# Up projection of a two-layer decoder trunk: three 256-column matmuls per weight tile in place of one of 512 and one of 256 columns

## The chip, the cores and the metric

The kernel runs on one core of a Trainium2 chip. The metric is the device time in microseconds (us). Before the change it is 2064.75 us, the median of three runs (2064.12 to 2065.49). Engine names are those of the profile: PE is the matrix engine's matmul row, PEld its weight loads, DVE is VectorE, ACT is ScalarE, POOL is GpSimd and SP the queue that issues most of the transfers.

## What is computed

A trunk of two layers on 256 tokens of width 2048, in float32. Each layer is a mixer (attention of one sort or another) with its residual add, and then this:

```python
def squared_relu_mlp(h, w_up, w_down):
    a = jnp.square(jax.nn.relu(h @ w_up))
    return a @ w_down

h = rmsnorm(x, ln_mlp_g[layer])
x = x + squared_relu_mlp(h, mlp_w_up[layer], mlp_w_down[layer])
```

`w_up` is 2048 x 8192 and `w_down` is 8192 x 2048. The change touches only `jnp.square(jax.nn.relu(h @ w_up))`.

## The kernel before

**Split operands.** The matrix engine is fed with a rounded float32 format (fp32r). To keep float32 precision each operand is split in a high part (the value rounded to that format) and a low part (what the rounding left). A product is then three matmuls: high by high, high by low and low by high. The low-by-low term is left out. In the mixer and in the down projection they are written as three matmuls of 512 columns (`piece_rows`, lines 1539 to 1541, and `product`, lines 1848 to 1850): there the activations are the stationary operand, 128 x 128, and 512 columns of weights stream.

**The up projection is the other way round** (`piece_cols`, lines 1599 to 1614): a 128 x 128 tile of the weights is stationary, and the activations stream: `h[:, k]` holds for one of the 16 slices `k` of the model dimension the high parts of 256 tokens and right behind them the low parts. The high weight tile is multiplied with all 512 columns (line 1609), so that high-by-high lands in the left half of a bank of PSUM and high-by-low in its right half. The low weight tile is multiplied with the 256 high columns only (line 1612), into the right half. The two halves of the bank are added later.

**Staging.** Each layer's MLP is cut in four blocks of 2048 hidden columns (`NB`), and the up stage of a block in four chunks `c` of 512 hidden columns. A chunk is eight pieces `j`, a piece has two slices `k`, and a slice four weight tiles `m`, taken in two groups of two (`COL_GROUPS`). So a chunk has 64 weight tiles, a block 256, and the kernel's eight blocks 2048. A chunk fills four banks, one for each `m`; two sets of four banks take turns (`up_set`).

**Behind a chunk.** ScalarE copies the four right halves to `s_buf` (`right_half`, line 966), VectorE adds the left halves to it (line 1471, which also frees the banks: `cols_read`), and takes relu and square in one operation (line 1473, `y_buf`). Then ScalarE rounds `y_buf` to the high part of `a` (line 1028) and VectorE makes the low part (line 1477), and the sums of tokens that the down projection uses follow (lines 1396 to 1401 on VectorE, line 1012 on ScalarE).

**What sets the order around it.** Every engine's program is written out by hand, and semaphores tie them. SP fetches a weight chunk of 1 MB into one of four raw slots. For each piece ScalarE makes the high half (`split_hi`, line 763) and VectorE the low half (`split_lo`, line 1068), four pieces ahead of the matmuls (`AHEAD`, as many as there are slots). PE waits for each piece on `lo_done`, and at the start of a chunk for the banks (`x_added` for chunks 0 and 1, `cols_read` of the chunk two before for chunks 2 and 3). The down stage follows with eight pieces of ordinary matmuls (chunk 0), a middle part of quads with summed weights for chunks 1 and 2, for which POOL issues the transfers (lines 678 and 687), and eight pieces more (chunk 3). Its first pieces wait for the low parts of `a` (`split_done`), four slices at a time. Everywhere the weight load of a matmul is an instruction of its own in the profile (PEld), with the matmul's line.

Of the kernel before, what the change touches and what calls it, by code (L numbers as in the profile page):

```python
# [27 lines left out]
ALU = mybir.AluOpType  # L28
ACT = mybir.ActivationFunctionType
# [3 lines left out]
T = 256  # L33
TT = T // P
D = 2048
KT = D // P
# [179 lines left out]
def up_set(c):  # L216
    return (c + 1) % 2
# [109 lines left out]
def build(nc, x, positions, ln_mix_g, ln_mlp_g, sf_w_in, sf_b_f, fox_q_g, fox_k_g, sf_w_o,  # L327
# [4 lines left out]
    with ExitStack() as ctx:  # L332
# [3 lines left out]
        def sem(name):  # L336
            return ctx.enter_context(nc.semaphore(name))
# [80 lines left out]
        s_buf = nat[:, 0].rearrange("p s (k t) -> p (s k) t", t=T)  # L418
        y_buf = nat[:, 1].rearrange("p s (k t) -> p (s k) t", t=T)
# [21 lines left out]
        psum = ctx.enter_context(nc.psum_tensor("psum", [P, 8, N], F32))  # L441
        SCORES, PROBS, OUT, TURN = psum[:, 4], psum[:, 5], psum[:, 6], psum[:, 7]
        X1, X2, X3, X4, X5, X6, X7, X8 = (psum[:, b] for b in (2, 6, 4, 7, 0, 5, 1, 3))

        def head_bank(n):

            return TURN if n % 16 >= 12 and n % 2 else OUT
# [9 lines left out]
        pieces_used = sem("pieces_used")  # L457
        r_ready = sem("r_ready")
        rows_read, cols_read = sem("rows_read"), sem("cols_read")
        right_read = sem("right_read")  # L460
        consts = sem("consts")
        const_step = sem("const_step")
        x_turned, h_hi = sem("x_turned"), sem("h_hi")
# [1 line left out]
        y_done, y_hi = sem("y_done"), sem("y_hi")  # L465
# [55 lines left out]
        def half_piece(n, which):  # L521
            kts, width = shape_of(n)
            if narrow(n):
                return narrow_piece(n)[:, :, which]
            return halves[:, n % SLOTS, which, 0:N if PIECES[n][0] == "b22" else flat(kts, width)]
# [217 lines left out]
        def _(act):  # L743
# [216 lines left out]
                        act.wait_ge(out_ready, n - 1)  # L960
                    nc.scalar.copy(o_buf[:, n % 2], head_bank(n)[:, 0:T]).then_inc(out_copied, 1)

            def right_half(set_, end):

                act.wait_ge(pieces_used, end)
                nc.scalar.copy(s_buf, psum[:, 4 * set_:4 * set_ + 4, T:2 * T]).then_inc(right_read, 1)

            def mixer(chunks, start, rows_no, norm):
                n = start
# [44 lines left out]
            def mlp_block(layer, b0):  # L1014

                base, no = block_base(layer, b0), block_no(layer, b0)
                for c in range(4):

                    for j in range(7):
                        split_hi(base + 8 * c + j + AHEAD)  # L1020
                        if c == 1 and j == 3:
                            token_sums_hi(no, 1)
                        if b0 == 0 and c == 0 and j == 2:
                            turned_x(2 * layer + 1, 3, out_bank(3))
                    right_half(up_set(c), base + 8 * c + 8)
                    split_hi(base + 8 * c + 7 + AHEAD)
                    act.wait_ge(y_done, (UP0, UP1)[layer] + 4 * b0 + c + 1)
                    nc.scalar.copy(a[:, 4 * c:4 * c + 4, 0, :], y_buf).then_inc(y_hi, 1)
                    token_sums_hi(no, c + 1 if c else 0)
                for j in range(32, BLOCK_PIECES):  # L1030
                    if base + j + AHEAD < P_END:
                        split_hi(base + j + AHEAD)
                    if j == 34:
                        token_sums_hi(no, 5)
                    for at, slot, bank in ((quad_at(7) - 1, 3, X8), (quad_at(7), 0, X1)):
                        if j == at:
                            act.wait_ge(pieces_used, base + at + 1)
                            act.wait_ge(lo_done, base + quad_at(FAST_QUADS[3]) + 2)
                            nc.scalar.copy(c_sum[:, slot], bank).then_inc(joint_copied, 1)
                    if layer == 0 and b0 == NB - 1 and j in LAST_TURNS:  # L1040
                        turned_x(2, LAST_TURNS.index(j), LAST_TURN_BANK[LAST_TURNS.index(j)])
# [12 lines left out]
        def _(dve):  # L1054
# [396 lines left out]
            def mlp_block(layer, b0):  # L1451

                base, no = block_base(layer, b0), block_no(layer, b0)
                up0 = (UP0, UP1)[layer] + 4 * b0
                for c in range(4):

                    for j in range(7):
                        split_lo(base + 8 * c + j + AHEAD)
                        if c and j == 1:
                            token_sums_lo(no, c if c > 1 else 0)  # L1460
                        if c == 1 and j == 2:
                            token_sums(no, 1)
                        if c == 1 and j == 4:
                            token_sums_lo(no, 1)
                        if b0 == 0 and c == 0 and j == 2:
                            h_split(2 * layer + 1, 3, out_bank(3))
                        if b0 == 0 and c == 1 and j == 2:
                            inverse_square(layer)
                    bank = 4 * up_set(c)
                    dve.wait_ge(right_read, up0 + c + 1)  # L1470
                    v.tensor_tensor(s_buf, psum[:, bank:bank + 4, 0:T], s_buf, ALU.add).then_inc(cols_read, 1)
                    dve.wait_ge(cols_read, up0 + c + 1)
                    v.scalar_tensor_tensor(out=y_buf, in0=s_buf, scalar=0.0, in1=s_buf, op0=ALU.max,
                                           op1=ALU.mult).then_inc(y_done, 1)
                    split_lo(base + 8 * c + 7 + AHEAD)
                    dve.wait_ge(y_hi, up0 + c + 1)
                    v.tensor_tensor(a[:, 4 * c:4 * c + 4, 1, :], y_buf, a[:, 4 * c:4 * c + 4, 0, :].bitcast(F32),
                                    ALU.subtract).then_inc(split_done, 1)
                    token_sums(no, c + 1 if c else 0)
                sums = {34: 0, 37: 1, quad_at(2) - 3: 2, quad_at(3) - 1: 3, quad_at(5) - 2: 4, quad_at(6) - 1: 5}  # L1480
                end = quad_at(8)
                joined = {end - 2: (1,), end - 1: (2, 3), end: (4, 5), end + 1: (6, 7), end + 2: (8, 9),
                          end + 3: (10, 11), end + 4: (12,)}
                ends = {39: 0, BLOCK_PIECES - 1: 3}
                for j in range(32, BLOCK_PIECES):
                    if j in ends:
                        c = ends[j]
                        final = layer == 1 and b0 == NB - 1 and c == 3
                        for tt in range(TT):
                            if final and tt == 0:  # L1490
                                dve.wait_ge(half_summed, 1)
                            else:
                                dve.wait_ge(pieces_used, base + j + 1)
                            ins = add_x(tt, c, psum[:, DOWN_BANK[c] + tt])
                            if final and tt == 0:
                                ins.then_inc(x_half, 1)
                        ins.then_inc(x_added, 1)
                    if base + j + AHEAD < P_END:
                        split_lo(base + j + AHEAD)
                    if j == 33:  # L1500
                        token_sums_lo(no, 4)
                        token_sums(no, 5)
                    if j == 35:
                        token_sums_lo(no, 5)
                    if j in sums:
                        weight_sums(layer, b0, sums[j])
                    for step in joined.get(j, ()):
                        combine(no, step, base)
                    if layer == 0 and b0 == NB - 1 and j in LAST_TURNS:
                        h_split(2, LAST_TURNS.index(j), LAST_TURN_BANK[LAST_TURNS.index(j)])  # L1510
# [14 lines left out]
        def _(pe):  # L1525
# [73 lines left out]
            def piece_cols(n, j, set_, src):  # L1599

                for i in range(2):
                    k = 2 * j + i
                    for group in COL_GROUPS:
                        for which in ((0, 1) if k == 0 else (1, 0)):
                            for m in group:
                                bank = psum[:, 4 * set_ + m]
                                cols = slice(i * N + m * P, i * N + (m + 1) * P)
                                if which == 0:
                                    last = mm(bank, half_piece(n, 0)[:, cols], src[:, k].rearrange("p s t -> p (s t)"),  # L1609
                                              start=(k == 0), stop=(k == KT - 1))  # L1610
                                else:
                                    last = mm(bank[:, T:2 * T], half_piece(n, 1)[:, cols], src[:, k, 0],  # L1612
                                              start=False, stop=False)
                return last


# [350 lines left out]
```

## Time and profile before

| | |
|---|---|
| median of three runs | 2064.75 us (2064.12 to 2065.49) |
| profiled execution, first to last instruction (span) | 2063.2 us |
| granted TensorE clock, mean | 1.000 |
| PE busy | 2056.0 us (100%), 10360 matmuls |
| PEld busy | 1745.4 us (85%) |
| DVE busy | 1455.9 us (71%) |
| ACT busy | 1099.2 us (53%) |
| HBM | 209 GB/s over the span |

For the profiled execution the profile gives no other time than its span; the span is 1.6 us under the median of the runs. Busy time of PE is taken from modelled ends: matmuls overlap in the record, so the distance from one matmul's start to the next is the figure to use for what one costs, and the "mean ns of one" of a matmul is not. Where the timeline merges several instructions of a line into one row (x2, x4), the row's time runs from the first start to the last end.

### The profile page before, as it was taken

Reading aid. Unit: us, or ns where it says so; the run is one execution under the profiler, and the core shown is the slowest. Engines: PE = TensorE matmul, PEld = TensorE weight load, DVE = VectorE, ACT = ScalarE, POOL = GpSimd, SP = SyncE. Lnnn points to the kernel's source line nnn. Section 1 sums busy time; section 2 is a strip of 40 time slices with the busy share of each in tenths; the row PEclk is TensorE's granted clock in tenths of the full one; section 3 lists DMA queues with packets and bytes.
Section 4 is the critical chain, followed back from the end, with each engine's and each line's share of the span. In section 5 each row is a group of like instructions: output and inputs, shape, how many; then the busy total and the mean of one; then the engine's idle time right before and its main releaser. Section 6 shows DMA issues by size and latency. Waiting matters only on the chain.

```text
span 2063.2 us, 26156 instructions
## 1 busy us (share of the span) xinstructions
PE 2056.0 (100%) x10360; PEld 1745.4 (85%) x10360; DVE 1455.9 (71%) x1957; ACT 1099.2 (53%) x1578; POOL 214.9 (10%) x317
## 2 busy tenths in 40 slices
PE   9999999999999999999999999999999999999999
PEld 7888888888888888888888898888888888888887
DVE  6556555566876876786697788557786696687777
ACT  5546565454544544554466676444554464454454
POOL 0000000020210120010010155001110021012010
PEclk9999999999999999999999999999999999999999
DMA  8544554685796796697575443568697588679565
GB/s 281 176 158 164 163 169 158 185 263 184 241 285 194 226 279 203 190 289 235 185 238 185 154 128 123 164 204 245 199 305 208 187 262 266 200 226 289 181 196 192
DMA packets 219986, 432.33 MB, mean 210 GB/s; under 512 B 13964, under 2 KB 20184, under 8 KB 219864
## 3 DMA queue, kind: packets, MB, share of 16 engines
q1 hardware_dynamic: 198312, 380.29, 55.5%
q0 software_dynamic: 21504, 50.34, 10.7%
q8 instruction: 83, 1.36, 0.3%
q14 instruction: 39, 0.32, 0.0%
q10 hardware_dynamic: 48, 0.02, 0.0%
HBM read 428.52 MB, written 2.10 MB: 209 GB/s over the span
## 4 chain that ended last, share of the span: by engine, by line
PE 98%; DVE 1%; ACT 0%; DMA 0%; issue 0%; SPq 0%; DVEq 0%; ACTq 0%
PE psum L1609 23%; PE psum L1539 14%; PE psum L1541 14%; PE psum L1540 14%; PE psum L1612 11%; PE psum L1850 5%; PE psum L1848 5%; PE psum L1849 5%; PE psum L1689 1%; PE psum L1776 1%; PE psum L1633 1%; PE psum L1753 0%; PE psum L1582 0%; PE psum L1777 0%; DMA raw<-in_sf_w_in 0%; PE psum L1733 0%
## 5 line engine op out<-in xcount | busy, mean ns | idle before, releaser
L1068 DVE TENSOR_TENSOR halves<-raw,halves 128x1024 fp32r<-128x1024 f32 (+1 forms) x724 | 849.9, 1181 | 447.4 <-ACT halves L763 443.3
L763 ACT CAST halves<-raw 128x1024 fp32r<-128x1024 f32 (+1 forms) x724 | 725.2, 1014 | 610.2 <-PE psum L1541 294.3
L1609 PE MATMUL psum<-h,halves 128*128 128x512 f32 x2048 | 639.0, 395 | 0.0
L1612 PEld LDWEIGHTS psum<-h,halves 128*128 128x128 f32 x2048 | 380.1, 188 | 87.6
L1612 PE MATMUL psum<-h,halves 128*128 128x256 f32 x2048 | 397.9, 278 | 0.0
L1539 PE MATMUL psum<-halves,a 128*128 128x512 f32 x828 | 325.4, 393 | 0.0
L1541 PE MATMUL psum<-halves,a 128*128 128x512 f32 x828 | 322.7, 390 | 0.0
L1540 PE MATMUL psum<-halves,a 128*128 128x512 f32 x828 | 322.3, 389 | 0.0
L1609 PEld LDWEIGHTS psum<-h,halves 128*128 128x128 f32 x2048 | 314.3, 189 | 2.8
L1539 PE MATMUL psum<-halves,h 128*128 128x512 f32 (+1 forms) x508 | 201.3, 396 | 1.0 <-DVE h L1139 1.0
L1541 PE MATMUL psum<-halves,h 128*128 128x512 f32 (+1 forms) x508 | 194.9, 384 | 0.0
L1540 PE MATMUL psum<-halves,h 128*128 128x512 f32 (+1 forms) x508 | 194.5, 383 | 0.0
L1541 PEld LDWEIGHTS psum<-halves,a 128*128 128x128 f32 x828 | 155.4, 188 | 32.8
L1539 PEld LDWEIGHTS psum<-halves,a 128*128 128x128 f32 x828 | 155.5, 188 | 31.7 <-ACT nat L830 0.4
L1540 PEld LDWEIGHTS psum<-halves,a 128*128 128x128 f32 x828 | 155.6, 188 | 31.5
L678 POOL DMA_DIRECT2D mix<-in_mlp_w_down x48 | 29.8, 637 | 1194.5 <-DVE halves L1068 1101.4
L1541 PEld LDWEIGHTS psum<-halves,h 128*128 128x128 f32 x508 | 95.3, 188 | 18.0
L1539 PEld LDWEIGHTS psum<-halves,h 128*128 128x128 f32 x508 | 95.5, 188 | 17.4 <-DVE halves L1068 1.2
L1540 PEld LDWEIGHTS psum<-halves,h 128*128 128x128 f32 x508 | 95.6, 188 | 16.2
L1849 PE MATMUL psum<-halves,a 128*128 128x512 f32 x272 | 105.8, 389 | 0.0
L1850 PE MATMUL psum<-halves,a 128*128 128x512 f32 x272 | 105.8, 389 | 0.0
L1848 PE MATMUL psum<-halves,a 128*128 128x512 f32 x272 | 105.8, 389 | 0.0
(268 smaller groups left out, 2095.9 us busy)
## 6 DMA issues: line engine op xcount, KB each, us to landing
raw<-in_mlp_w_up SPq DMA_DIRECT2D x128, 1024.0 KB, 6.3
raw<-in_mlp_w_down SPq DMA_DIRECT2D x128, 1024.0 KB, 5.3
mix<-in_mlp_w_down POOLq DMA_DIRECT2D x192, 256.0 KB, 7.0
raw<-in_sf_w_in SPq DMA_DIRECT2D x45, 1024.0 KB, 5.1
raw<-in_sf_w_o SPq DMA_DIRECT2D x16, 1024.0 KB, 5.1
raw<-in_mla_w_o SPq DMA_DIRECT2D x16, 1024.0 KB, 5.2
raw<-in_mla_w_down SPq DMA_DIRECT2D x8, 1024.0 KB, 5.3
raw<-in_mla_w_ukv SPq DMA_DIRECT2D x8, 1024.0 KB, 5.5
```

The costliest lines, as they stand in the source:

```text
L678: pool.dma_start(u[:, 0], b11).then_inc(u_loaded[m % 2], 16)
L763: nc.scalar.copy(half_piece(n, 0), raw_piece(n)).then_inc(hi_done, 1)
L1068: v.tensor_tensor(half_piece(n, 1), raw_piece(n), half_piece(n, 0).bitcast(F32), ALU.subtract)\
L1539: mm(bank, x_hi, hi[:, i], start=(k == 0), stop=False)
L1540: mm(bank, x_hi, lo[:, i], start=False, stop=False)
L1541: last = mm(bank, x_lo, hi[:, i], start=False, stop=(k == total_kts - 1))
L1609: last = mm(bank, half_piece(n, 0)[:, cols], src[:, k].rearrange("p s t -> p (s t)"), start=(k == 0), stop=(k == KT - 1))
L1612: last = mm(bank[:, T:2 * T], half_piece(n, 1)[:, cols], src[:, k, 0], start=False, stop=False)
L1633: ins = nc.tensor.transpose(psum[:, bank + i // 2, col:col + P], x_tok[:, tt, k * P:(k + 1) * P], ident[:])
L1848: mm(bank, x_hi, w_hi, start=start, stop=False)
L1849: mm(bank, x_hi, w_lo, start=False, stop=False)
L1850: return mm(bank, x_lo, w_hi, start=False, stop=stop)
```

## The change

Each weight tile is now multiplied by three matmuls of 256 columns, all into the same 256 columns of PSUM: high weights by high activations, high weights by low activations, low weights by high activations. The two tiles of a group share one bank (two times 256 columns), so a chunk takes two banks instead of four. Only the first matmul into a bank carries the start flag. ScalarE reads the result through a relu (and so frees the banks), VectorE squares what ScalarE wrote, and the operation that added the halves is gone.

```diff
+        def up_bank(set_):
+
+            return psum[:, 4 * set_:4 * set_ + 2].rearrange("p b (m t) -> p (b m) t", t=T)
...
-            def right_half(set_, end):
+            def rectify(set_, end):
 
                 act.wait_ge(pieces_used, end)
-                nc.scalar.copy(s_buf, psum[:, 4 * set_:4 * set_ + 4, T:2 * T]).then_inc(right_read, 1)
+                nc.scalar.activation(s_buf, up_bank(set_), ACT.Relu).then_inc(cols_read, 1)
...
-                    right_half(up_set(c), base + 8 * c + 8)
+                    rectify(up_set(c), base + 8 * c + 8)
...
-                    bank = 4 * up_set(c)
-                    dve.wait_ge(right_read, up0 + c + 1)
-                    v.tensor_tensor(s_buf, psum[:, bank:bank + 4, 0:T], s_buf, ALU.add).then_inc(cols_read, 1)
                     dve.wait_ge(cols_read, up0 + c + 1)
-                    v.scalar_tensor_tensor(out=y_buf, in0=s_buf, scalar=0.0, in1=s_buf, op0=ALU.max,
-                                           op1=ALU.mult).then_inc(y_done, 1)
+                    v.tensor_tensor(y_buf, s_buf, s_buf, ALU.mult).then_inc(y_done, 1)
...
                     for group in COL_GROUPS:
-                        for which in ((0, 1) if k == 0 else (1, 0)):
+                        for w, x in ((0, 0), (0, 1), (1, 0)):
                             for m in group:
-                                bank = psum[:, 4 * set_ + m]
+
+                                out = up_bank(set_)[:, m]
                                 cols = slice(i * N + m * P, i * N + (m + 1) * P)
-                                if which == 0:
-                                    last = mm(bank, half_piece(n, 0)[:, cols], src[:, k].rearrange("p s t -> p (s t)"),
-                                              start=(k == 0), stop=(k == KT - 1))
-                                else:
-                                    last = mm(bank[:, T:2 * T], half_piece(n, 1)[:, cols], src[:, k, 0],
-                                              start=False, stop=False)
+                                last = mm(out, half_piece(n, w)[:, cols], src[:, k, x],
+                                          start=(k == 0 and m == group[0] and (w, x) == (0, 0)),
+                                          stop=(k == KT - 1 and m == group[-1] and (w, x) == (1, 0)))
```

## Rows read from the trace of the kernel before

**Rows 1.** The page: span, busy time, the chain that ended last by engine.

```profile
span 2063.2 us, 26156 instructions
PE 2056.0 (100%) x10360; PEld 1745.4 (85%) x10360; DVE 1455.9 (71%) x1957; ACT 1099.2 (53%) x1578; POOL 214.9 (10%) x317
PE 98%; DVE 1%; ACT 0%; DMA 0%; issue 0%; SPq 0%; DVEq 0%; ACTq 0%
```

**Rows 2.** Windows: one up stage, then one down stage (engines' busy time, clock, DMA).

```profile
581.65:670.86 89.21, 89.21 (x513) 77.88 (x512) 57.59 (x65) 40.97 (x42) 5.06 (x7) 1.00 0.71 220
670.86:753.86 83.00, 83.00 (x367) 68.72 (x366) 70.58 (x82) 46.42 (x50) 12.12 (x17) 1.00 0.78 244
```

**Rows 3.** Waits of PE (waiter, releaser: us in total, times, longest).

```profile
PE psum L1620 <- POOL ident L631: 1.6, 1, 1.6
PE psum L1539 <- DVE h L1139: 1.0, 1, 1.0
PE psum L1689 <- DVE mix L1239: 0.6, 1, 0.6
PE psum L1689 <- DVE mix L1262: 0.4, 1, 0.4
```

**Rows 4.** Timeline, PE in an up stage (start us, us, engine, line).

```profile
584.66 0.62 PE L1609 MATMUL psum<-h,halves 128*128 128x512 f32 x2
...
601.85 0.40 PE L1612 MATMUL psum<-h,halves 128*128 128x256 f32 x2
602.08 0.63 PE L1609 MATMUL psum<-h,halves 128*128 128x512 f32 x2
602.55 0.39 PE L1612 MATMUL psum<-h,halves 128*128 128x256 f32 x2
602.78 0.62 PE L1609 MATMUL psum<-h,halves 128*128 128x512 f32 x2
```

**Rows 5.** Timeline, PE: a run of 384-column matmuls in the second mixer.

```profile
1159.50 0.33 PE L1539 MATMUL psum<-halves,h 128*128 128x384 f32 x1
...
1161.41 0.33 PE L1541 MATMUL psum<-halves,h 128*128 128x384 f32 x1
```

**Rows 6.** Timeline, PE: four 256-column matmuls in a row, in two chunks.

```profile
409.75 0.63 PE L1612 MATMUL psum<-h,halves 128*128 128x256 f32 x4
410.21 0.62 PE L1609 MATMUL psum<-h,halves 128*128 128x512 f32 x2
...
432.92 0.64 PE L1612 MATMUL psum<-h,halves 128*128 128x256 f32 x4
433.40 0.62 PE L1609 MATMUL psum<-h,halves 128*128 128x512 f32 x2
```

**Rows 7.** Timeline, weight loads: sixteen before matmuls of only 8 columns.

```profile
161.76 1.86 PEld L1593 LDWEIGHTS psum<-ident,nat 16*128 16x128 f32 x16
```

**Rows 8.** Timeline, PE: 512-column matmuls after short ones in the first mixer.

```profile
89.36 0.40 PE L1540 MATMUL psum<-halves,h 128*128 128x512 f32 x1
...
90.98 0.39 PE L1541 MATMUL psum<-halves,h 128*128 128x512 f32 x1
```

**Rows 9.** Timeline, ACT behind a chunk of the up stage.

```profile
431.96 1.01 ACT L966 COPY nat<-psum 128x1024 f32<-128x1024 f32 x1 [1.68 <-PE psum L1609]
435.53 1.05 ACT L1028 CAST a<-nat 128x1024 fp32r<-128x1024 f32 x1 [1.60 <-DVE nat L1473]
```

**Rows 10.** Timeline, DVE behind the same chunk.

```profile
433.01 1.22 DVE L1471 TENSOR_TENSOR nat<-psum,nat 128x1024 f32<-128x1024 f32 x1 [1.47 <-ACT nat L966]
434.27 1.23 DVE L1473 SCALAR_TENSOR_TENSOR nat<-nat 128x1024 f32<-128x1024 f32 x1
435.41 1.22 DVE L1068 TENSOR_TENSOR halves<-raw,halves 128x1024 fp32r<-128x1024 f32 x1
436.61 1.23 DVE L1477 TENSOR_TENSOR a<-nat,a 128x1024 fp32r<-128x1024 f32 x1
```

**Rows 11.** Groups by line on ACT: the table loads.

```profile
L775 ACT ACT_TABLE_LOAD x1 | 1.3, 1283 | 1.3 <-PEq L1957 1.3
L998 ACT ACT_TABLE_LOAD x1 | 1.3, 1283 | 0.0
```

More of the change, by code:

```diff
@@ L459, in build @@
         rows_read, cols_read = sem("rows_read"), sem("cols_read")
-        right_read = sem("right_read")
         consts = sem("consts")
```

## Prediction

> **What bounds the kernel now.** I read the page first: PE is busy for the whole span and makes 98% of the chain of work that ended last, while DVE stands at 71% and ACT at 53% [rows 1]. Busy time of PE alone proves little, so I read the waits next. PE waits for 3.6 us in all, in the start and in the mixers, and not once in an up stage [rows 3]. The granted clock is 1.00 in the up and in the down stage, the higher of the two levels, 2.4 GHz [rows 2]. So in the up stage nothing but the matrix engine's own stream counts. What an edit takes off DVE or ACT is worth nothing there, and what it adds to a matmul is paid in full.
>
> The price of a matmul is the distance between starts, not its duration in the record. Before the change one up stage lasts 89.21 us [rows 2]; it has 256 weight tiles, so one tile, a 512-column and a 256-column matmul, costs **348.5 ns**. The timeline says the same: from the pair of 512s at 584.66 to that at 602.78 are 26 repeats of two 512s and two 256s, 18.12 / 26 = 697 ns for two tiles [rows 4]. There are eight such stages: 8 x 256 = 2048 tiles, 713.7 us, a third of the kernel.
>
> **The change, part by part.**
>
> *The matmuls.* The streamed columns stay the same, 768 per tile. At 2.4 GHz they take 320 ns, so 28.5 ns of a tile is something else: 14 ns for each of its two matmuls. The change makes three matmuls and three weight loads of it. Everything hangs on what a 256-column matmul costs in an unbroken stream of its kind, which this trace does not have. Four readings bound it.
>
> (a) A down stage, only 512-column matmuls, has 366 in 83.00 us, 226.8 ns each [rows 2]. A run of 384-column ones has 11 steps in 1.91 us, 173.6 ns each [rows 5]. The difference is 53.2 ns for 128 columns, near the 53.3 of the clock, so on top of the columns there is a fixed part of about 13 ns a matmul. Carried to 256 columns: 173.6 - 53.2 = 120.4 ns.
>
> (b) At the first slice of each chunk four 256-column matmuls stand in a row: 0.46 us in one chunk and 0.48 us in the next, for four [rows 6]. That is 115 and 120 ns each, 117.5 on average. A row of four leans on its neighbours at both ends, so it is not a steady rate.
>
> (c) The remainder of the mix: 697 less two 512s at 226.8 leaves 243.4 for two 256s, 121.7 ns each. This is the upper end of what I take as likely.
>
> (d) In the mix itself a pair of 256s goes from 602.55 to 602.78, and one from 601.85 to 602.08: 115 ns each [rows 4]. It is the lower end. The 512s beside them (602.08 to 602.55 for two) then take 235 ns, more than in (a), so part of the 256s' cost seems to stand in their gaps.
>
> I take **119 ns**, the middle between (a) and (b), which are nearest to the new stream: the one is a steady stream of another width, the other the right width without being steady. Three of them make 357.0 ns a tile, 8.5 ns more than now; times 2048 this is **+17.4 us**. With (b) alone it is 352.5, +4.0 ns, +8 us; with (c) 365.1, +16.6 ns, +34 us.
>
> The Trainium skill, "TensorE: Matmul & The Clock Gate", section "Back-to-back issue gap", gives for a stream of warm matmuls the columns over 2.4 plus 2.5 ns. By that a 512 costs 215.8 and a 256 109.2 ns, a third matmul adds 2.5 ns a tile, and the change would cost only 5.1 us, an estimate of 2069.9 us. This case's trace does not agree: its 512s stand 226.8 ns apart [rows 2], so the measured fixed part goes into the sum.
>
> *The weight loads.* 2048 more of them. Sixteen loads before matmuls too short to matter take 1.86 us from the first start to the last end; less one load's own 0.19 us (as the others on the timeline show) that is 15 steps of 111 ns [rows 7]. A 256-column matmul that takes 117 to 121 ns covers this, by 6 to 10 ns only. Before the change every second load had a 512 over it. I cost it at nothing; if the cover failed, the load's distance would be the floor.
>
> *Accumulation in one place.* The same 256 columns of PSUM are now added to at every second matmul. In the down stage consecutive matmuls add to the same bank at 226.8 ns with no sign of a stall [rows 2]; cost nothing. The two banks that come free are not used by anybody.
>
> *ScalarE.* The copy of 1.01 us [rows 9] becomes a relu of as many elements; I take 1.01 to 1.1 us. It now frees the banks itself, 1.3 us earlier than the add does. PE waits for them only one chunk (22 us) later and does not wait today, so nothing is gained.
>
> *VectorE.* The add, 1.22 us, goes; the square takes 1.22 like the operation it replaces [rows 10]. 32 chunks x 1.22 = 39 us less DVE busy time. The chain behind a chunk (copy, add, square, round, low half) gets about 1.25 us shorter. Who needs its end? The down stage, whose seventh piece is the first to read the last chunk's slices, 6 pieces of 12 matmuls at 226.8 ns = 16.3 us after the chunk's end; the chain today is through 5.9 us after the copy starts (431.96 to 436.61 + 1.23). Nothing waits for it, so both savings are worth nothing; if a run should show PE waiting there, that cover was misjudged. VectorE's wait is now on ScalarE's relu in place of ScalarE's copy, at the same point of its program; the low half of a weight piece is queued behind it, as it was, and PE has pieces in hand.
>
> *Sum.* The profiled execution has 2063.2 us of span; 2063.2 + 17.4 = 2080.6. The median of the runs lies 1.6 us above that span, so I predict **2082.2 us**.
>
> **The rivals.**
>
> *The 256s cost what they show in the mix (same).* If the 115 to 116 ns of (d) are a true rate, three of them are 345 to 348 ns against 348.5, and the kernel stays at 2064.75 less 0 to 7 us; at 116 it is 2063.7. For it: all the pairs of the up stage show it. Against: then the 512s beside them would cost 8 ns more than in a down stage, without a reason. Chance 0.12.
>
> *The load distance rules (faster).* In a stream of equal 256s there is no 512 to disturb the rhythm, and the matmul could follow the next load at 111 ns [rows 7]. A tile then takes 334 ns, 14.6 less, and the kernel 29.9 us less: 2034.9. It decides from 116.2 ns a matmul downwards, today's tile over three. For it: the four in a row come down to 115 in one sighting. Against: it would need the fixed 13 ns of (a) to shrink to less than 5. Chance 0.08. The skill's same page, section "LDWEIGHTS (loading the stationary operand)", puts a load at its 128 columns over 1.2, 107 ns, whatever the matmul; the trace's 111 ns distance is near that.
>
> *A broken rhythm (much slower).* After short matmuls the 512s run for a while at 231 ns (seven steps in 1.62 us) before they settle at 227 [rows 8]. If loads that are only just covered keep the stream in that state, a 256 costs 120.4 + 4.6 = 125 ns, a tile 375, and the kernel +54 us: 2119. The price is paid at every matmul. For it: the load's cover is thin. Against: the four in a row. Chance 0.07.
>
> *Relu is not in the loaded table set.* Then the change does not simply swap a copy for a relu: a table load costs 1283 ns [rows 11], and where log and exp tables alternate with it there would be some. Even two a chunk, 82 us in all, would go on an ACT that is busy 41 of 89 us in an up stage [rows 2], and PE would not feel it. It changes ACT's row, not the time. Chance that it shows in the time 0.02.
>
> **How the numbers follow.** The forecast's own case, a fixed part per matmul with 117 to 122 ns for a 256, has 0.71 and runs from 2072 to 2100 us. The range takes in this and the first rival, 2063 to 2101; left out are the load distance and the broken rhythm, 0.15 together. A measurement of this kernel can tell 0.2%, 4.1 us, from no change. Slower by more: 0.71 and 0.07, 0.78. Faster by more: 0.08 from the load distance and 0.01 from the lower edge of the first rival, 0.09. The same: 0.11 from the rest of that rival and 0.02 from the tables, 0.13.
>
> **What would show it.** In the changed profile an up stage (89.21 us before) should last 256 x 0.357 = 91.4 us, the three new groups of the up line together 6144 matmuls about 119 ns apart, and the down stage its 83.0 us as before. PE should still wait for nothing in the up stages. DVE's busy time should fall by 39 us, ACT's stay within 5 us, and the chain behind a chunk be one operation shorter. The count of table loads should stay at three. I am wrong if the up stage is at or under 89.2 us (the cost is not per matmul), if the matmuls stand 111 to 113 ns apart, or if the added time lies anywhere else than in the up stages.

## Result and profile after

The changed kernel takes **2091.09 us** (median of four runs, 2089.8 to 2094.23), the kernel before, run beside it, 2065.12. The ratio is 1.0129, with a 95% interval of 1.0117 to 1.0141: 26.0 us slower. That is in the predicted range and of the predicted sign, but 8.6 us over the predicted sum of 17.4.

The page of the changed kernel: span, busy time, and the chain that ended last by engine.

```profile
span 2088.9 us, 30220 instructions
PE 2080.7 (100%) x12408; PEld 1860.1 (89%) x12408; DVE 1420.8 (68%) x1925; ACT 1102.9 (53%) x1578; POOL 214.9 (10%) x317
PE 97%; DMA 1%; DVE 1%; ACT 1%; issue 0%; POOL 0%; ACTq 0%; POOLq 0%; DVEq 0%
```

There are 2048 more matmuls and loads than in [rows 1], and DVE has lost 35 us. The matrix engine is still the chain, with one new thing in it: 1% DMA.

Windows of the same up stage and the down stage behind it, in the changed kernel:

```profile
586.11:678.26 92.15, 92.15 (x769) 92.15 (x768) 54.41 (x62) 41.20 (x42) 5.26 (x8) 1.00 0.70 215
678.26:761.25 82.99, 82.99 (x369) 68.70 (x367) 69.75 (x82) 46.69 (x50) 12.32 (x18) 1.00 0.78 244
```

The up stage has 92.15 us against 89.21 [rows 2], the down stage is the same. 92.15 us over 256 tiles is 360.0 ns a tile, over 768 matmuls **120.0 ns** each. Weight loads are now in flight for all of the stage. One chunk's timeline shows the stream without a break:

```profile
454.73 10.48 PE L1608 MATMUL psum<-h,halves 128*128 128x256 f32 x86
```

Over eight stages, 2.94 us more each, that is 23.5 us. The spans of the two profiles differ by 25.7 us (2063.2 and 2088.9), so 2.2 us are left. They lie in the first and the third down stage, 2.2 and 0.6 us longer than before, with small differences elsewhere. There the matrix engine has waits of a kind that it had nowhere before [rows 3]:

```profile
PE psum L1538 <- DVE halves L1071: 2.1, 2, 1.9
PE psum L1617 <- POOL ident L634: 1.6, 1, 1.6
PE psum L1686 <- DVE mix L1242: 0.6, 1, 0.6
PE psum L1686 <- DVE mix L1265: 0.4, 1, 0.4
```

The first line is new; on the other side the wait of 1.0 us for `h` [rows 3] is not in this profile. The timeline of PE at the end of the first block's down stage shows the longer of its two waits:

```profile
572.59 0.39 PE L1539 MATMUL psum<-halves,a 128*128 128x512 f32 x1
572.81 0.39 PE L1540 MATMUL psum<-halves,a 128*128 128x512 f32 x1
575.05 0.50 PE L1538 MATMUL psum<-halves,a 128*128 128x512 f32 x1 [1.85 <-DVE halves L1071]
```

From 572.81 to 575.05 are 2.24 us in place of 0.23; at the other place, two blocks later, 0.61 us stand in place of 0.23, so the two cost 2.4 us. VectorE is named, but it waited for ScalarE, and ScalarE for a transfer. ACT at that place in the changed kernel:

```profile
572.70 1.99 ACT L766 CAST halves<-raw 128x1024 fp32r<-128x1024 f32 x2 [8.96 <-DMA raw<-in_mlp_w_down]
```

And in the kernel before:

```profile
568.03 2.00 ACT L763 CAST halves<-raw 128x1024 fp32r<-128x1024 f32 x2 [6.56 <-DMA raw<-in_mlp_w_down]
```

There too ScalarE waited for that load. VectorE's low half of the piece, and the first matmul that needed it, in the kernel before:

```profile
569.12 1.23 DVE L1068 TENSOR_TENSOR halves<-raw,halves 128x1024 fp32r<-128x1024 f32 x1 [4.40 <-ACT halves L763]
```

```profile
570.77 0.39 PE L1539 MATMUL psum<-halves,a 128*128 128x512 f32 x1
```

The piece was ready at 570.35 (569.12 + 1.23) and the matrix engine came to it at 570.77: in time by 0.4 us. In the changed kernel the engine would have come to it at 573.04 (572.81 + 0.23), 2.3 us later, but the load landed 4.7 us later (572.70 against 568.03). Why it lost 2.4 us more than the stages moved isn't shown. In both kernels POOL's transfers for the next block run beside it; here in the changed kernel:

```profile
558.22 0.54 POOL L681 DMA_DIRECT2D mix<-in_mlp_w_down  x1 [5.24 <-DVE halves L1071]
...
559.27 1.85 POOL L690 DMA_DIRECT2D mix<-in_mlp_w_down  x2
563.63 1.76 POOL L690 DMA_DIRECT2D mix<-in_mlp_w_down  x2 [2.51 <-DMA mix<-in_mlp_w_down]
```

Behind a chunk, DVE in the changed kernel:

```profile
433.07 1.22 DVE L1473 TENSOR_TENSOR nat<-nat 128x1024 f32<-128x1024 f32 x1 [1.58 <-ACT nat L969]
434.21 1.22 DVE L1071 TENSOR_TENSOR halves<-raw,halves 128x1024 fp32r<-128x1024 f32 x1
435.41 1.23 DVE L1476 TENSOR_TENSOR a<-nat,a 128x1024 fp32r<-128x1024 f32 x1
```

The add of [rows 10] is gone and the low half of `a` starts 2.34 us after the square instead of 3.60 us after the add: the chain is shorter by one operation, as planned. What that is worth is measured below ("The evacuation alone"). ScalarE's groups show the relu at 1025 ns where the copy took 1013 to 1016, and there are still three table loads in all (two of them here):

```profile
L969 ACT ACTIVATE nat<-psum 128x1024 f32<-128x1024 f32 x32 | 32.8, 1025 | 56.9 <-PE psum L1608 56.9
L778 ACT ACT_TABLE_LOAD x1 | 1.3, 1283 | 1.3 <-PEq L1954 1.3
L1001 ACT ACT_TABLE_LOAD x1 | 1.3, 1283 | 0.0
```

### The profile page after: what moved, and what is told of

It reads as the page before. It is cut to its first block, busy times and chain, and to the rows that moved or that the text cites. A ratio compares the mean times of both kernels' runs of the same rounds, so it can differ in the third digit from the quotient of the medians.

```text
span 2088.9 us, 30220 instructions
## 1 busy us (share of the span) xinstructions
PE 2080.7 (100%) x12408; PEld 1860.1 (89%) x12408; DVE 1420.8 (68%) x1925; ACT 1102.9 (53%) x1578; POOL 214.9 (10%) x317
## 4 chain that ended last, share of the span: by engine, by line
PE 97%; DMA 1%; DVE 1%; ACT 1%; issue 0%; POOL 0%; ACTq 0%; POOLq 0%; DVEq 0%
PE psum L1608 35%; PE psum L1538 14%; PE psum L1540 14%; PE psum L1539 14%; PE psum L1846 5%; PE psum L1845 5%; PE psum L1847 5%; DMA raw<-in_mlp_w_down 1%; PE psum L1686 1%; PE psum L1773 1%; PE psum L1630 1%; DVE halves L1071 0%; PE psum L1750 0%; PE psum L1581 0%; PE psum L1774 0%; PE psum L1730 0%
## 5 line engine op out<-in xcount | busy, mean ns | idle before, releaser
L766 ACT CAST halves<-raw 128x1024 fp32r<-128x1024 f32 (+1 forms) x724 | 728.4, 1013 | 678.1 <-PE psum L1540 297.3
L1608 PE MATMUL psum<-h,halves 128*128 128x256 f32 x6144 | 739.0, 283 | 0.0
L1608 PEld LDWEIGHTS psum<-h,halves 128*128 128x128 f32 x6144 | 738.4, 192 | 0.6
L681 POOL DMA_DIRECT2D mix<-in_mlp_w_down x48 | 29.8, 638 | 1218.3 <-DVE halves L1071 1123.7
L690 POOL DMA_DIRECT2D mix<-in_mlp_w_down x96 | 86.5, 1079 | 119.3 <-DMA mix<-in_mlp_w_down 118.8
L766 ACT CAST halves<-heads 128x1024 fp32r<-128x1024 f32 x48 | 50.5, 1053 | 45.9 <-PE psum L1847 19.2
```

Of the source, the lines that this page charges most:

```text
L681: pool.dma_start(u[:, 0], b11).then_inc(u_loaded[m % 2], 16)
L690: pool.dma_start(u[:, i], b12, accum_op=ALU.add).then_inc(u_summed[m % 2], 16)
L766: nc.scalar.copy(half_piece(n, 0), raw_piece(n)).then_inc(hi_done, 1)
L1608: last = mm(out, half_piece(n, w)[:, cols], src[:, k, x], start=(k == 0 and m == group[0] and (w, x) == (0, 0)), stop=(k == KT - 1 and m = ...
```

## Experiments

Two theories stood against each other at the start. Mine: every matmul carries a fixed part of 13 ns and the third one is all that costs. The other: the time comes with what else is new, the accumulation in one place and one bank, or the work of ScalarE and VectorE.

### The split alone

The banks, the add and everything else stay as before; only the 512 columns go in two matmuls.

```diff
                                 if which == 0:
-                                    last = mm(bank, half_piece(n, 0)[:, cols], src[:, k].rearrange("p s t -> p (s t)"),
-                                              start=(k == 0), stop=(k == KT - 1))
+                                    for x in range(2):
+                                        last = mm(bank[:, x * T:(x + 1) * T], half_piece(n, 0)[:, cols], src[:, k, x],
+                                                  start=(k == 0 and x == 0), stop=(k == KT - 1 and x == 1))
```

> The kernel before with its 512-column matmul of each weight tile split into two of 256 columns, into the same left and right halves of the same four banks; ScalarE's copy, VectorE's add and the rest stay. If the added time is a fixed part of each matmul (my theory), the up line stands 120 ns apart as in the changed kernel, the up stages take 737 us in all against 714, and the time is 2086 to 2092 us. If the time comes from adding up in one place of PSUM, or from two tiles in one bank, it is gone here: 2065 us, with 116 ns steps. If it comes from the new ScalarE and VectorE operations, it is gone too: 2065 us.

Measured: 2090.09 us, ratio 1.0123 (1.011 to 1.0137). One up stage of it (window), then its waits and the timeline of PE around the late load:

```profile
588.23:680.38 92.15, 92.15 (x770) 92.15 (x768) 56.58 (x63) 41.04 (x42) 3.65 (x5) 1.00 0.69 210
```

```profile
PE psum L1539 <- DVE halves L1068: 2.1, 1, 2.1
```

```profile
575.58 0.50 PE L1539 MATMUL psum<-halves,a 128*128 128x512 f32 x1 [2.15 <-DVE halves L1068]
575.91 0.58 PE L1540 MATMUL psum<-halves,a 128*128 128x512 f32 x1
...
577.15 0.63 PE L1540 MATMUL psum<-halves,a 128*128 128x512 f32 x1
577.58 0.63 PE L1541 MATMUL psum<-halves,a 128*128 128x512 f32 x1
```

The same 92.15 us, and the same wait at the same place. So the loss comes with the split, 25.4 us here against 26.0 in the change; one place in PSUM, relu and square have no measurable part in it. In this profile the granted clock fell behind the wait: the 512s stand 0.43 us apart instead of 0.23, and the clock of that stretch is 0.50, the 1.2 GHz level, where it was 1.00 before the wait:

```profile
576.00:579.00 3.00, 3.00 (x9) 2.32 (x8) 2.96 (x5) 2.00 (x2) 0.00 (x0) 0.50 1.02 379
```

Seven matmuls start in these 3 us, where thirteen would at 226.8 ns. The changed kernel's own profile has the wait without the fall. And the fall doesn't need the wait: the profile of the next run, "The evacuation alone", has one at 163.94 us, in the first mixer, where the engine waited for nothing but had run, from 160.99 us on, sixteen matmuls of 8 columns:

```profile
160.99 1.95 PE L1588 MATMUL psum<-ident,nat 16*128 16x8 f32 x16
```

```profile
164.00:167.30 3.30, 3.30 (x10) 2.56 (x9) 1.67 (x6) 0.65 (x3) 0.00 (x0) 0.50 0.12 44
```

The kernel before has the same sixteen matmuls [rows 7] and no fall in its profile. Such falls are a likely part of the spread between single runs, of the kernel before too (2064.12 to 2066.07 us); that the slowest run of the change (2094.23 us, mean clock 0.999) had one is not shown.

### The evacuation alone

```diff
-                nc.scalar.copy(s_buf, psum[:, 4 * set_:4 * set_ + 4, T:2 * T]).then_inc(right_read, 1)
+                nc.scalar.activation(s_buf, psum[:, 4 * set_:4 * set_ + 4, T:2 * T], ACT.Relu).then_inc(cols_read, 1)
...
-                    dve.wait_ge(right_read, up0 + c + 1)
-                    v.tensor_tensor(s_buf, psum[:, bank:bank + 4, 0:T], s_buf, ALU.add).then_inc(cols_read, 1)
...
-                    v.scalar_tensor_tensor(out=y_buf, in0=s_buf, scalar=0.0, in1=s_buf, op0=ALU.max,
-                                           op1=ALU.mult).then_inc(y_done, 1)
+                    v.tensor_tensor(y_buf, s_buf, s_buf, ALU.mult).then_inc(y_done, 1)
```

> The kernel before with the matmuls untouched, but ScalarE reads the right halves through a relu and frees the banks, VectorE's add is left out and it squares with a product. The left halves are not added, so high-by-high is missing from the result. My theory: all of this is hidden behind the matrix engine; 2065 us within 2, with 39 us less DVE busy time and the up stages unchanged at 714 us. Rival: the shorter chain behind a chunk or the earlier free banks help, 2060 us or less; or the relu costs table loads and time, over 2069 us.

Measured: 2064.63 us, ratio 0.9999 (0.999 to 1.0008). The result lacks high by high, so only its time counts. Its window of the up stage, and its page:

```profile
582.52:671.73 89.21, 89.21 (x514) 77.91 (x512) 54.27 (x62) 41.37 (x42) 5.14 (x7) 1.00 0.72 221
```

```profile
PE 2057.7 (100%) x10360; PEld 1747.4 (85%) x10360; DVE 1420.3 (69%) x1925; ACT 1104.1 (53%) x1578; POOL 215.0 (10%) x317
```

89.21 us to the hundredth, with 36 us less on VectorE. That half of the change is worth nothing here, neither way.

### Half of the slices

```diff
-                                if which == 0:
-                                    last = mm(bank, half_piece(n, 0)[:, cols], src[:, k].rearrange("p s t -> p (s t)"),
-                                              start=(k == 0), stop=(k == KT - 1))
+                                if which == 0 and k % 2:
+                                    for x in range(2):
+                                        last = mm(bank[:, x * T:(x + 1) * T], half_piece(n, 0)[:, cols], src[:, k, x],
+                                                  start=False, stop=(k == KT - 1 and x == 1))
+                                elif which == 0:
+                                    last = mm(bank, half_piece(n, 0)[:, cols], src[:, k].rearrange("p s t -> p (s t)"),
+                                              start=(k == 0), stop=False)
```

> The kernel before with the 512-column matmul split into two of 256 in every second slice only: half the added matmuls of the split alone. A fixed part per matmul is paid by the piece: the up stages gain 11.8 us (three of 120 ns against 348.5 in half the tiles), 726 us in all, and the time is 2076 to 2079 us. If the added time came from a lost rhythm that needs an unbroken stream of 256s, it would be under 5 us; if mixing widths costs more by itself, over 15 us.

Measured: 2076.92 us, ratio 1.0062 (1.0046 to 1.0077), 12.1 us over the kernel before at its side. Its window of an up stage:

```profile
582.84:673.49 90.65, 90.65 (x642) 84.97 (x640) 57.85 (x65) 41.12 (x42) 5.31 (x8) 1.00 0.70 219
```

1.44 us more than before, 2.94 for all slices: half the added matmuls, half the time. The price is per added matmul, and an unbroken stream of 256s is not needed for it.

### How near is the weight load?

```diff
-                                    last = mm(bank[:, T:2 * T], half_piece(n, 1)[:, cols], src[:, k, 0],
-                                              start=False, stop=False)
+                                    for t in range(2):
+                                        last = mm(bank[:, T + t * P:T + (t + 1) * P], half_piece(n, 1)[:, cols],
+                                                  src[:, k, 0, t * P:(t + 1) * P], start=False, stop=False)
```

> The kernel before with the 256-column matmul of the low weights split into two of 128 columns: the same number of matmuls as in the changed kernel. If only the fixed part of 13 ns counts, a tile is 226.8 + 2 x 66.6 = 360 ns and the time 2089 us. If weight loads can't follow each other faster than 111 to 112 ns, a tile is 226.8 + 2 x 112 = 451 ns, 102 more than now, and the time about 2275 us; then the 256-column matmuls of the change are 8 ns clear of that floor. If part of a load hides under the 512 beside it, between the two.

Measured: 2286.59 us, ratio 1.1077 (1.1062 to 1.1092). Two rows of its timeline are one pattern, four 128-column matmuls and two of 512. Behind them stand the weight loads of the first pattern's 128s and of the next two 512s:

```profile
499.60 0.68 PE L1609 MATMUL psum<-h,halves 128*128 128x512 f32 x2
500.12 0.56 PE L1613 MATMUL psum<-h,halves 128*128 128x128 f32 x4
500.52 0.68 PE L1609 MATMUL psum<-h,halves 128*128 128x512 f32 x2
...
501.43 0.68 PE L1609 MATMUL psum<-h,halves 128*128 128x512 f32 x2
```

```profile
499.89 0.65 PEld L1613 LDWEIGHTS psum<-h,halves 128*128 128x128 f32 x4
500.45 0.30 PEld L1609 LDWEIGHTS psum<-h,halves 128*128 128x128 f32 x2
```

From 499.60 to 501.43 are two patterns, 1.83 / 4 = 457 ns a tile. Less 226.8 for the 512 it leaves 115 ns for each 128-column matmul, where the fixed part alone would give 66.6. The two loads of the last row take 0.30 us; less one load's own 0.19 that is 0.11 us from start to start. Taken singly, the loads of this run's up projection stand 108 to 112 ns apart wherever nothing holds them longer, and none is closer. So a second limit stands beside the fixed part, the distance of the loads. The 256s of the change lie above it, 120.0 against 112, but a 128-column split falls on it: as many matmuls as the change, and 222 us lost, not 24.

### One place, back to back

```diff
-                        for w, x in ((0, 0), (0, 1), (1, 0)):
-                            for m in group:
+                        for m in group:
+                            for w, x in ((0, 0), (0, 1), (1, 0)):
```

> The changed kernel with its three matmuls of a tile one behind the other: each adds to the same 256 columns as the one before, and the high weight tile is loaded twice in a row. If accumulation into one place costs nothing even back to back and a repeated load is neither saved nor dearer, all steps stay at 120 ns and the time at 2091 us within 2. If a matmul must wait for the one before it at the same address, steps grow by tens of ns, over 2110 us. If the repeated load were left out, a step of every three would be shorter than 120 ns, under 2085 us.

Measured: 2091.18 us, ratio 1.0129 (1.0116 to 1.0143). Its window of an up stage and its weight loads as a group:

```profile
584.01:676.17 92.16, 92.16 (x770) 92.15 (x768) 54.06 (x62) 41.22 (x42) 4.94 (x7) 1.00 0.70 215
```

```profile
L1608 PEld LDWEIGHTS psum<-h,halves 128*128 128x128 f32 x6144 | 738.4, 192 | 0.6
```

Adding to the place the matmul before wrote costs nothing, and the same weights are loaded a second time: 6144 loads, none left out. The late load of the change is in this profile too, at two other block ends (2.6 us in all, the longer 2.38 us from start to start), and no fall of the clock.

### The late weight load

The transfers that POOL issues early for the next block now wait until the block before is through. The same edit was made in the changed kernel and in the kernel before.

```diff
-                    pool.wait_ge(lo_done, base - BLOCK_PIECES + quad_at(FAST_QUADS[m + 4]) + 2)
+                    pool.wait_ge(lo_done, base)
```

> The changed kernel, but the first summed-weight transfers that POOL issues for a block wait until the last piece of the block before has been split, so they no longer run beside the last down-projection chunk's own loads. The changed kernel's profile has 23.5 us more in its up stages and 2.4 us of waits of the matrix engine for a late weight load at two block ends. If those waits come from the two streams of transfers sharing the DMA engines, they are gone here: 2088.5 us, 1.5 to 3 us less than the change, and the distances of the up line stay at 120 ns. If they come from elsewhere (a slot freed late, the longer up stage itself), the time stays at 2090 to 2092 us.

> The same edit in the kernel before, which shows no such wait in its profile. 2064.7 us within 1.5, unless its other runs hold waits that the profiled one hasn't: then up to 1 us less. If the later transfers come too late for VectorE's weight sums instead, more than 2067 us.

Measured: 2087.79 us for the change with the edit (2087.62 to 2088.28, ratio to before 1.0113, 1.0099 to 1.0127), and 2064.39 for the kernel before with it (0.9999, 0.999 to 1.0008). The timeline of ACT in the edited change, where the wait was:

```profile
568.19 1.05 ACT L766 CAST halves<-raw 128x1024 fp32r<-128x1024 f32 x1 [1.61 <-PE psum L1540]
570.97 1.05 ACT L766 CAST halves<-raw 128x1024 fp32r<-128x1024 f32 x1 [1.72 <-PE psum L1540]
```

The transfers between 555 and 575 us, first in the changed kernel and then in the edited one (queue: packets, MB, share of the 16 DMA engines; and a load of 1 MB, median us from issue to landing). q0 is missing where POOL issues nothing, so it has POOL's transfers:

```profile
q0 software_dynamic: 793, 1.73, 41.8%
q1 hardware_dynamic: 1339, 2.68, 36.7%
raw<-in_mlp_w_down SPq DMA_DIRECT2D x2, 1024.0 KB, 14.1
```

```profile
q1 hardware_dynamic: 2469, 4.93, 69.6%
raw<-in_mlp_w_down SPq DMA_DIRECT2D x2, 1024.0 KB, 6.2
```

And the window of the up stage in the edited change:

```profile
584.31:676.47 92.16, 92.16 (x770) 92.15 (x769) 53.01 (x60) 41.20 (x42) 8.62 (x12) 1.00 0.74 222
```

ScalarE waits for the matrix engine again and not for a transfer, and the matrix engine has no such wait left. The change now costs 22.9 us against the kernel before at its side, and 23.4 against the kernel before with the same edit: the 23.5 us of its matmuls and no more. The interval of this ratio overlaps with that of the change, so the time alone is weak evidence; but all four runs lie under the fastest of the change (2089.8 us), and the profile has no late load. So the rest, some 3 us of 26, came from POOL's transfers beside the due loads: with them on the DMA engines a load of 1 MB took 14.1 us to land, without them 6.2. The kernel before doesn't gain; in its profile that load was just in time.

### Two attempts to beat both

Steady streams of 226.8 and 120.0 ns would make 346.8 ns a tile, where the kernel before takes 348.5. Two orders of the same matmuls were tried for it. Runs of eight:

```diff
-COL_GROUPS = ((0, 1), (2, 3))
+COL_GROUPS = ((0, 1, 2, 3),)
...
-                        for which in ((0, 1) if k == 0 else (1, 0)):
+                        for which in ((0, 1) if k % 2 == 0 else (1, 0)):
```

> The kernel before with all four tiles of a slice in one group and the order high/low turned round from slice to slice, so that eight matmuls of one width stand in a row where two did; the matmuls are the same. In the kernel before, two 512s and two 256s take 697 ns where steady streams (226.8 and the 120.0 of the changed kernel) would take 693.6. If each change of width costs 1.7 ns, three fewer a slice over 512 slices take off 2.6 us: 2062.5 us, up stages 711 us. If a 256 beside 512s simply costs 121.7 however they are ordered, nothing changes: 2065 us, 714 us.

Measured: 2065.86 us, ratio 1.0006 (0.9997 to 1.0015). One by one:

```diff
-                        for which in ((0, 1) if k == 0 else (1, 0)):
-                            for m in group:
+                        for m in group:
+                            for which in ((0, 1) if k == 0 else (1, 0)):
```

> The kernel before with the two matmuls of a tile one behind the other, so that 512 and 256 columns take turns singly (low weights first, then high), where they took turns in pairs; the matmuls are the same. Runs of eight did not lower the up stages (715 us against 714), because the 512s after a change of width run 5 to 10 ns over their steady 226.7 for several matmuls. If that surcharge needs a few equal matmuls to build up, single turns come nearer to the steady sum of 346.7 ns a tile: up stages about 711 us, the time 2062 to 2063 us, and this would beat both kernels. If every change of width costs the same, twice the changes cost 3.5 us more: 2068 us. If the mix costs 697 ns for two tiles whatever its order, 2065 us.

Measured: 2073.07 us, ratio 1.0044 (1.003 to 1.0058). The windows of an up stage, runs of eight and then one by one:

```profile
581.20:670.58 89.38, 89.38 (x513) 78.66 (x512) 57.71 (x65) 41.01 (x42) 5.18 (x7) 1.00 0.71 221
```

```profile
581.55:671.98 90.43, 90.43 (x514) 78.45 (x512) 57.45 (x64) 41.09 (x42) 4.89 (x7) 1.00 0.70 217
```

The timeline of the runs of eight:

```profile
599.82 2.00 PE L1609 MATMUL psum<-h,halves 128*128 128x512 f32 x8
601.66 1.12 PE L1612 MATMUL psum<-h,halves 128*128 128x256 f32 x8
602.61 2.00 PE L1609 MATMUL psum<-h,halves 128*128 128x512 f32 x8
```

Eight 256s take 0.95 us, 119 ns each, but the eight 512s 1.84, 230 ns each, 3 over their steady rate. Both expectations of a gain fell, and 2073 us lies above all three cases that the last one named. Mixing has a price over 346.8 ns: 1.7 ns a tile in pairs, 2.3 in eights (89.38 / 256 = 349.1), and 6.4 one by one (353.2). It is no fixed price for each change of width: eights have a quarter of the changes of pairs and cost no less. The pairs of the kernel before are the best of the three, and none of the versions tried is faster than it. What in the engine makes the 512s slower after a change of width stays open.

## Why the prediction was right, and where it fell short

**The bound** was right for the up stage: there nothing counts but the matrix engine's stream, and the third matmul is paid in full. The evacuation alone at 0.9999 shows it for the other half of the change.

**The price of a 256** was taken as 119 ns, the middle between reading (a), two steady streams of other widths, 120.4, and reading (b), four in a row, 117.5. It is 120.0. Reading (a) was right and needed no averaging. A row of 256s beside 512s is no steady rate: in the runs of eight the 256s stand 119 ns apart while the 512s take 3 ns more. The step "I take 119" is the mis-sized term: 11.5 ns a tile instead of 8.5, 23.5 us instead of 17.4. Reading (a) alone would have given 12.7 ns a tile and 26.0 us, the measured total to the tenth, but by luck: 2.5 us of it would have stood for the late loads. A slip beside it: 117 to 122 ns give 2070 to 2101 us by the prediction's own sum, where it has 2072 to 2100; the result is inside both.

**Reading (c)**, 121.7, blamed the 256s for what is a price of mixing widths, which the change removes. And reading (d), with the rival that hung on it, took a start-to-start gap inside a mix for a rate: 115 ns beside 512s, 120.0 alone. The 8 ns more of the 512s, held against that rival as being without a reason, are real; what causes them stays open.

**"Cost nothing" for accumulation in one place**, for the relu and for the square: right, each by its own run. DVE lost 35 us and not 39. Its operations' own times, added up, fell by 37.0; back-to-back operations overlap a little in the record (434.27 to 435.41 is 1.14 us for one of 1.23 [rows 10]), and busy time counts the overlap once. The other 2 us stay open. The table loads stayed at three.

**The load distance.** The rival of a faster stream at 111 ns fell: in the unbroken stream the 256s stand 120.0 ns apart. So did the rival of a broken rhythm, which had 125. But the load distance is real, and the run with the low weights' matmul in two of 128 columns shows it, 108 to 112 ns between loads and 115 for a matmul. The Trainium skill has 107 ns for a load of 128 columns ("TensorE: Matmul & The Clock Gate", "LDWEIGHTS (loading the stationary operand)"); the 108 to 112 ns here are near it and a little above. The same page, "Back-to-back issue gap", has the columns over 2.4 plus 2.5 ns, which this section calls the gap of an isolated matmul; taken for the rate of this stream it is an estimate of 5.1 us for the change. The measured part over the columns at 256 is 120.0 - 106.7 = 13.3 ns, and the measurement decides.

**The missed part.** I wrote that the down stage stays, and that I am wrong if the added time lies anywhere else than in the up stages. That sign came true for some 3 us of 26: in the profile the matrix engine waited for weights at the ends of two of the eight down stages. The waits list of the kernel before could not show this, since it lists only what was late, and that load was early by 0.4 us. The hint lay one engine further on: ScalarE's own wait of 6.56 us for the same load. In "Sum" nothing stood for a transfer, and some 3 us were due. So of the 8.6 us over the sum, 6.1 are the size of a 256, and the rest is the late loads.

## What to carry to other kernels

Where the matrix engine is the bound, count matmuls as well as columns: in this format each one carried 13.3 ns beside its columns, so a 512 split in two cost 13 ns more. Pieces of 128 columns fell on the distance of the weight loads: the same number of matmuls then cost nine times as much (222 us against 23.5). Take such a price from steady streams of two widths and a line through them, not from gaps inside a mix. And before calling other engines' slack free, look how long they wait for transfers themselves: here ScalarE waited 6.6 us for a load, and the piece behind it was ready only 0.4 us before the matrix engine came to it.

## What the runs showed of the hardware beyond that

A 256-column fp32r matmul with a new weight tile each time repeats every 120.0 ns, 512 columns every 226.8, 384 every 173.6 [rows 2, 5]. Loads of 128 columns follow each other at 108 to 112 ns at best in the up stages. Repeating the same weight tile saves nothing, and accumulating back to back into the same columns costs nothing. Mixing the two widths costs 1.7 to 6.4 ns a tile by the order, least in pairs. Plain loads of 1 MB took 14.1 us to land beside POOL's accumulating transfers and 6.2 without them. The granted clock fell to 0.50 for about 3 us behind a pause of 2.54 us from start to start in one profile, not behind pauses of 2.24 and 2.38 us in two others, and in a fourth with no pause at all, 3 us after the start of sixteen matmuls of 8 columns.
